# Decoder layer on one core: the order of SyncE's loads in three bodies, the first output chunks, and the last token block by halves

## What is computed

```python
h = rmsnorm(x, ln_gain[l])
z = jnp.einsum('bsd,de->bse', h, w_in[l])
q, k, v, g_attn, x_lru, g_lru = jnp.split(z, SPLITS, axis=-1)
q = partial_rope(q.reshape(b, s, N_Q_HEADS, HEAD_DIM), cos, sin)
k = partial_rope(k.reshape(b, s, N_KV_HEADS, HEAD_DIM), cos, sin)
...
y_attn = rmsnorm(y_attn * jax.nn.silu(g_attn), attn_out_gain[l])
u = causal_depthwise_conv(x_lru, conv_w[l], conv_b[l])
y_lru = rg_lru(u, w_rgate[l], b_rgate[l], w_igate[l], b_igate[l], lru_lambda[l])
y_lru = rmsnorm(y_lru * jax.nn.silu(g_lru), lru_out_gain[l])
y = jnp.einsum('bse,ed->bsd', jnp.concatenate([y_attn, y_lru], axis=-1), w_out[l])
x = x + y
...
return rmsnorm(x, final_gain)
```

## Time and profile before

| | |
|---|---|
| median of 3 runs | 1440.1 us (1439.48 to 1441.57) |
| profiled execution | 1439.82 us, span 1438.2 us |
| PE busy | 1380.8 us (96%), 6464 products |
| DVE / ACT / POOL busy | 1014.2 (71%) / 769.1 (53%) / 316.1 (22%) |
| clock granted to PE, mean | 0.993 |

### The profile page before, as it was taken

The page is one execution under the profiler, slowest core; times in us unless marked ns, Lnnn a source line. Parts: engine busy times, 40 slices in busy tenths (PEclk is TensorE's granted clock), DMA queues, the critical chain, the costliest instruction groups (busy, mean ns, idle before and its releaser), DMA issues.

```text
span 1438.2 us, 21776 instructions
## 1 busy us (share of the span) xinstructions
PE 1380.8 (96%) x6464; PEld 1136.5 (79%) x6464; DVE 1014.2 (71%) x1729; ACT 769.1 (53%) x1552; POOL 316.1 (22%) x317
## 2 busy tenths in 40 slices
PE   5999999799999999999999999999989999999997
PEld 4778777688888888888888878788868888888886
DVE  4798989687877778787787868777886644344443
ACT  5677685747475664747566564747575322222221
POOL 2131423042322314232231414232230000000000
PEclk9999999999999999999999999999999999999999
DMA  8767674755546454554636374544717323233220
GB/s 221 243 240 246 237 248 162 253 202 193 182 155 197 157 198 165 176 185 154 222 120 235 126 244 151 194 160 167 231 53 257 119 86 117 73 102 101 74 87 29
DMA packets 151726, 243.24 MB, mean 169 GB/s; under 512 B 35440, under 2 KB 101232, under 8 KB 151664
## 3 DMA queue, kind: packets, MB, share of 16 engines
q1 hardware_dynamic: 144496, 217.33, 45.4%
q0 software_dynamic: 7168, 25.17, 5.2%
HBM read 179.55 MB, written 62.91 MB: 169 GB/s over the span
## 4 chain that ended last, share of the span: by engine, by line
PE 43%; DVE 21%; issue 18%; ACT 8%; POOL 3%; DMA 2%; SPq 2%; DVEq 1%; ACTq 1%; POOLq 0%
PE ring L1408 18%; PE acc_b L201 12%; PE ring L201 11%; DVE hs L1283 5%; POOL ri L618 2%; DVE p_lo L1220 2%; ACT p_sb L834 2%; DVE s_sb L1194 2%; DVE smax L1207 1%; PE ps_v L1458 1%; DVE cu L1249 1%; DVE o_sb L1229 1%; ACT cu L858 1%; DVE w_lo L1002 1%; ACT kc_ol L847 1%
## 5 line engine op out<-in xcount | busy, mean ns | idle before, releaser
L1408 PE MATMUL ring<-split,w_hi 128*128 128x512 f32 x2304 | 720.3, 394 | 8.1 <-DVE split L1022 7.5
L1408 PEld LDWEIGHTS ring<-split,w_hi 128*128 128x128 f32 x2304 | 427.9, 189 | 95.6 <-DVE split L1022 8.4
L1408 PE MATMUL ring<-split,w_lo 128*128 128x512 f32 x1152 | 450.8, 391 | 0.0
L1408 PEld LDWEIGHTS ring<-split,w_lo 128*128 128x128 f32 x1152 | 217.2, 189 | 46.7
L834 ACT ACTIVATE p_sb<-s_sb,smax 128x129 f32<-128x129 f32 x256 | 99.9, 392 | 124.6 <-DVE smax L1207 124.4
L618 POOL TENSOR_TENSOR ri<-ri,hs 128x512 f32<-128x512 f32 x32 | 54.8, 1732 | 395.6 <-ACT hs L900 395.6
L774 ACT ACTIVATE q_st<-qrot 64x512 fp32r<-64x512 f32 x64 | 40.4, 631 | 114.9 <-DVE qrot L1085 114.1
L1249 DVE SCALAR_TENSOR_TENSOR cu<-xl,prm,cu 128x512 f32<-128x512 f32 x96 | 72.2, 752 | 39.6 <-ACT cu L858 30.6
L1669 ACT ACTIVATE w_hi<-res 128x1024 fp32r<-128x1024 f32 x16 | 17.0, 1061 | 144.5 <-DVE res L1728 144.5
L201 PE MATMUL ring<-split,y_own 128*128 128x512 f32 x384 | 91.3, 392 | 0.0
L201 PE MATMUL acc_b<-wo_rest,y_own 128*128 128x512 f32 x384 | 89.8, 390 | 0.5 <-DVE wo_rest L162 0.5
(11 more groups left out here) (195 smaller groups left out, 2486.0 us busy)
## 6 DMA issues: line engine op xcount, KB each, us to landing
w_hi<-w_split_scratch SPq DMA_DIRECT2D x108, 512.0 KB, 3.3
w_lo<-w_split_scratch SPq DMA_DIRECT2D x108, 512.0 KB, 4.3
w_split_scratch<-w_hi SPq DMA_DIRECT2D x36, 512.0 KB, 5.0
w_split_scratch<-w_lo SPq DMA_DIRECT2D x36, 512.0 KB, 5.7
w_raw<-w_in_d SPq DMA_DIRECT2D x32, 512.0 KB, 4.4
y_scratch<-hs POOLq DMA_DIRECT2D x32, 256.0 KB, 5.0
y_scratch<-ya POOLq DMA_DIRECT2D x16, 512.0 KB, 8.7
rows<-y_scratch SPq DMA_DIRECT2D x8, 1024.0 KB, 7.5
```

Source lines behind the costliest of these rows:

```text
L1408: last = mm(bank(r), w[:, i % WSLOTS, k, :], h[:, par, k, :], start=(k == 0 and j == 0), stop=(k == KC - 1 and j == 2))
```

## The change

Four things move. (1) In SP's list the four gate loads come directly behind XL1, ahead of `load_y(0, 0)` and the output weights; and the tables with their wait come behind GA0, GA1 and GL1. (2) In the four split bodies `norm_x` comes ahead of `softmax_a(1)` on DVE. (3) In the last body the gaps take three chunks of block 0, then the fourth and two of block 1, then two more of block 1: eight in place of six; phase B's beginning has two fewer. (4) The last step of phase B is taken out of the loops and its second block is worked by halves of 512 columns: the recurrence's product, the add, the square sum, the scaling and the store, which goes out from SP in two transfers and no longer from POOL. An unused split and square sum of a further y block, which the loop made in its last step, is gone with it.

```diff
@@ SP, phase A, body @@
                 load(XL1, COL_XL + P)
+                sp.wait_ge(*gw_low.at(n, 0))
+                for j, w in enumerate((w_rgate, w_igate)):
+                    for half in range(2):
...
+                                     ).then_inc(*gw_dma.one())
                 if q == NQUART - 1 and g == 0:
...
-                sp.wait_ge(*gw_low.at(n, 0))
-                for j, w in enumerate((w_rgate, w_igate)):
...
+                load(GA0, COL_GA)
+                load(GA1, COL_GA + P)
+                load(GL1, COL_GL + P)
                 if nxt_par != par and not last:
                     sp.wait_ge(*q_rot.at(n, 0))
                     load_tables((q + 1) * T)
-                load(GA0, COL_GA)
-                load(GA1, COL_GA + P)
-                load(GL1, COL_GL + P)
@@ DVE, phase A, body @@
                 if split:
                     split_w(n, GL1)
+                    norm_x(n, x_root.at(n, 1), x_rs, x_norm)
                 softmax_a(1)
                 if q < NQUART - 1:
-                    norm_x(n, x_root.at(n, 1), x_rs, x_norm)
+                    if not split:
+                        norm_x(n, x_root.at(n, 1), x_rs, x_norm)
@@ PE, phase A, last body @@
                     pe.wait_ge(*signals_b.y_low.at(0, 1))
-                    for e in range(2):
+                    for e in range(3):
                         pe.wait_ge(*signals_b.wo_low.at(e, 1))
                         proj.chunk(pe, ring, 0, e)
                 weigh_v(1)
...
-                    for e in range(2, 4):
-                        pe.wait_ge(*signals_b.wo_low.at(e, 1))
-                        proj.chunk(pe, ring, 0, e)
+                    pe.wait_ge(*signals_b.wo_low.at(3, 1))
+                    proj.chunk(pe, ring, 0, 3)
+
+                    pe.wait_ge(*ring_act.at(n, FREED_BY_ACT.index(R_I1) + 1))
+                    pe.wait_ge(*ring_dve.at(n, FREED_BY_DVE.index(R_GL1) + 1))
+                    pe.wait_ge(*signals_b.y_low.at(0, 2))
+                    for e in range(2):
+                        proj.chunk(pe, ring, 1, e)
                 weigh_v(2)
                 turn_p(3)
...
-                    for e in range(2):
+                    for e in range(2, 4):
                         proj.chunk(pe, ring, 1, e)
                 weigh_v(3)
@@ PE, phase B, beginning @@
             begin(4)
             begin(5)
-            for e in range(2, 4):
-                second(e)
-                begin(e + 4)
+            begin(6)
             second(4)
+            begin(7)
             second(5)
@@ phase B, last block: SP, ACT, DVE, PE @@
+            for h in range(2):
+                sp.wait_ge(b.half_normed, h + 1)
+                cols = slice(h * (D // 2), (h + 1) * (D // 2))
+                sp.dma_start(out[0, SEQ - P:, cols], res[:, 1, cols]).then_inc(b.half_out, 16)
+            sp.wait_ge(b.half_out, 32)
...
+            for h in range(2):
+                act.wait_ge(b.half_added, h + 1)
+                nc.scalar.activation(junk[:, h * (D // 2):(h + 1) * (D // 2)], res[:, 1, h * (D // 2):(h + 1) * (D // 2)],
+                                     ACT.Square, accum_out=stat[:, h, 0:1]).then_inc(b.half_sq, 1)
+            act.wait_ge(b.half_mean, 2)
...
+            for h, cols in enumerate(halves):
+                dve.wait_ge(b.half_product, h + 1)
+                stt(out=res[:, 1, cols], in0=acc_of(1, 1)[:, h, :], scalar=rms[:, 1, 2, 1:2], in1=res[:, 1, cols],
+                    op0=ALU.mult, op1=ALU.add).then_inc(b.half_added, 1)
...
+            step(STEPS - 1, 1, EC // 2)
+
+            pe.wait_ge(*b.y_mean.at(STEPS - 1, 4))
+            for h in range(2):
+                for e in range(EC // 2, EC):
+                    last = proj.multiply(pe, acc, 1, e, (h,))
+                last.then_inc(b.half_product, 1)
```

More of the change, by code:

```diff
@@ L195, in sum_y, with multiply @@
             ins.then_inc(*(self.b.y_part if half == 1 else self.b.y_tree).one())
-    def chunk(self, pe, banks, s, e):
+    def multiply(self, pe, banks, s, e, halves):
         g = e // (EC // 2)
         for j, (y, low) in enumerate(((self.y_hi, 0), (self.y_hi, 1), (self.y_lo, 0))):
-            for h in range(2):
+            for h in halves:
                 last = self.nc.tensor.matmul(banks[:, ACC[s, g][h], :], y[s][:, e, :],
@@ L204, in chunk @@
                                              stop=(e % (EC // 2) == EC // 2 - 1 and j == 2))
+        return last
+    def chunk(self, pe, banks, s, e):
+        last = self.multiply(pe, banks, s, e, range(2))
         if (e + 1) % (EC // 2) == 0:
@@ L1590, in signals_of_phase_b @@
     sem = lambda name: top.enter_context(nc.semaphore(name))
+    (b.half_product, b.half_added, b.half_sq, b.half_mean, b.half_root, b.half_normed, b.half_out) = (
+        sem("half_" + s) for s in ("product", "added", "sq", "mean", "root", "normed", "out"))
     b.over, b.fgain_in, b.settled = sem("phase_a_over"), sem("fgain_in"), sem("settled_b")
@@ L1767, in _, with step @@
             normalise(0, 1)
-            with dve.Fori(1, STEPS) as m:
-                for s in range(2):
-                    mean_y(m, s)
-                    proj.low_y(dve, m + s, 1 - s)
-                    rms_y(m, s)
-                    for g in range(2):
-                        proj.sum_y(dve, m + s, 1 - s, g)
-                    for g in range(2):
-                        add_group(m, s, g)
-                    normalise(m, s)
+            def step(m, s):
+                mean_y(m, s)
+                proj.low_y(dve, m + s, 1 - s)
+                rms_y(m, s)
+                for g in range(2):
+                    proj.sum_y(dve, m + s, 1 - s, g)
+                for g in range(2):
+                    add_group(m, s, g)
+                normalise(m, s)
+            with dve.Fori(1, STEPS - 1) as m:
+                for s in range(2):
+                    step(m, s)
+            m = STEPS - 1
+            step(m, 0)
+            mean_y(m, 1)
+            rms_y(m, 1)
+            add_group(m, 1, 0)
+            dve.wait_ge(*b.added.at(m, 3))
+            halves = [slice(h * (D // 2), (h + 1) * (D // 2)) for h in range(2)]
+            for h, cols in enumerate(halves):
+                dve.wait_ge(b.half_product, h + 1)
+                stt(out=res[:, 1, cols], in0=acc_of(1, 1)[:, h, :], scalar=rms[:, 1, 2, 1:2], in1=res[:, 1, cols],
+                    op0=ALU.mult, op1=ALU.add).then_inc(b.half_added, 1)
+                dve.wait_ge(b.half_sq, h + 1)
+                if h == 0:
+                    nc.vector.tensor_scalar(stat[:, 0, 1:2], stat[:, 0, 0:1], 1.0 / D, EPS, ALU.mult, ALU.add
+                                            ).then_inc(b.half_mean, 1)
+                else:
+                    dve.wait_ge(b.half_mean, 1)
+                    nc.vector.tensor_scalar(stat[:, 1, 1:2], stat[:, 1, 0:1], 1.0 / D, stat[:, 0, 1:2], ALU.mult, ALU.add
+                                            ).then_inc(b.half_mean, 1)
+            dve.wait_ge(b.half_root, 1)
+            nc.vector.reciprocal(stat[:, 1, 3:4], stat[:, 1, 2:3]).then_inc(b.half_root, 1)
+            dve.wait_ge(b.half_root, 2)
+            for cols in halves:
+                stt(out=res[:, 1, cols], in0=res[:, 1, cols], scalar=stat[:, 1, 3:4], in1=fgain[:, cols],
+                    op0=ALU.mult, op1=ALU.mult).then_inc(b.half_normed, 1)
         @block.tensor
```

69 lines of the change are left out of this document (36 added, 33 removed).

## The result

The changed kernel took 1425.04 us (median of four runs, 1424.16 to 1425.95) beside 1439.84 for the kernel before: ratio 0.990, 95% interval 0.9888 to 0.9912, or 14.8 us less. The forecast was 11.5 us less, 1428.6, with a range down to 1426.1. The kernel was measured again beside the last experiments: 1423.74 (1423.06 to 1426.38).

What follows compares the result with a forecast made beforehand. PE, busy 1380.8 of 1438.2 us, was taken as the bound, so its removed waits shorten the time. Terms -7.5 - 2.8 + 0.2 + 0.4 - 1.8 = -11.5 from 1440.1 gave 1428.6 us, range 1426.1 to 1432.8.

Steps and rivals of the forecast that it cites:

- part 5: Tail: last block by halves, stored from SP, shortens the end behind the last product; -1.8 us, bounds -1.0 and -2.3.
- part 2: Body 12: gate loads first remove PE's wait and slow clock, GA0's weights then slightly late; gain 2.8 us, bounds 1.2 and 4.1.
- part 1: Body 3: tables behind GA0, GA1 and GL1 remove two gate-product waits and the slow clock; -7.5 us, low end 5.9.
- Part 3: Split bodies: norm_x ahead of softmax_a(1) only moves PE's wait from turn_x to block 0's v product; +0.2 us.
- part 4: Last body: early chunks buy nothing and block 2's v product comes 0.4 later; +0.4 us, bounds -0.1 and +0.9.
- the 1.6 for the clock: Body 3: granted clock 0.73 over 6 us behind the long wait loses 1.6 us, which returns with the wait.
- (c): Bodies 3, 7 and 11: tables come too late, holding VectorE's first rotation and the key product; above 1443 us; 2%.
- (d): Body 3: GA0's load finds its slot still taken, ACT waits as before, gain 1 and not 7.5; 1435.1 us; 5%.
- small waits: Body 12: 0.5 us taken off the gain because bodies 13 to 15 show small waits at their v products.
- (b): Body 12: GA0's weights take the gate weights' place and eat the whole gain there; 1431.4 us; 15%.
- my own test: Split bodies: if block 0's v product does not wait longer (about 1.3 us), VectorE is not the bound there.
- (a): Last body: early chunks count if output weights come in time, giving -2.1 and not +0.4; 1426.1 us; 12%.

Runs made afterwards that it cites:

- alone: Kernel before with only one part of the change; parts 1 to 5 in order: 1431.5, 1436.79, 1439.7, 1441.04 and 1437.06 us.
- the kernel with the gate loads in the middle: Changed kernel, in body 12 the four gate loads behind load_y(0, 0) and ahead of the three output weights: 1424.98 us.

## Why the prediction was right or wrong

The time lies below the range because three terms of the sum were too small: part 5 by 1.5 us, part 2 by 1.4 and part 1 by 1.0. Part 3 had its sign wrong, and part 4 held.

**Part 1: right in cause and place, 1.0 too small.** Forecast -7.5, measured -8.45 alone. The waits to the first gate product gave 4.30 (forecast 4.14). Between the gate products went 3.63, where I had 1.95 - 0.21 + 1.6 = 3.34: I kept body 2's wait of 0.21 as a floor, and body 3 now has none (6.87 us between its gate products, 7.24 in body 2). And turn_x waits 0.70 and not 1.10, in a stretch that is 0.5 shorter, which I had not counted. One term was right by its sum and not by its reason: the 1.6 for the clock. In the seven profiles with the tables in their old place the stretch between the two gate products took 10.44 to 10.50 us, whether the clock in it was 0.71 or 0.85, with PE waiting 0.53 us or 1.95. DVE's u_lo sets this stretch, and a lower clock only fills the wait. Wait and lost clock together measure how late u_lo was, so the sum came out near; a "low end with no clock regained" had no ground. The kernel with the tail alone, with its wait of 0.53, to be laid beside the 10.50 us of the earlier trace rows:

```profile
264.94:275.38 10.44, 9.92 (x30) 7.59 (x30) 6.94 (x13) 8.47 (x14) 0.00 (x0) 0.71 0.74 277
```

The tables cost nothing, in bodies 7 and 11 either. Rivals (c) and (d) fall.

**Part 2: right in the wait, wrong in the step behind it.** Forecast -2.8, measured -4.16 alone and -4.26 in the whole: the full 2.42 + 1.7 that the earlier trace rows show. Here the clock's part was time: from the first gate product to the v product of block 3 body 12 took 45.44 before and 43.77 after. The step that failed is that the y load goes out about 2.5 us later, "so GA0 comes 0.1 to 2.2 us late; I take 0.8". GA0 came 1.2 us earlier against the work of PE (19.8 and not 21.0 behind the same v product). The y load did go out 2.6 us later, but I had carried its delay through to GA0: SP's issues behind it stood less (one took 3.81 us before, none over 1.3 after), so GA0 was issued 2.9 us earlier. Nor does an issue set the landing: in the kernel with the gate loads in the middle GA0 was issued 3.3 us later than in the changed kernel and landed 0.3 earlier. Nor did the 0.5 of "small waits" come off: bodies 13 to 15 have theirs as before, in either kernel, and body 12 none. Rival (b) has its mechanism, 0.41 us of wait in one profile of six, and not its price.

**Part 3: wrong in place and sign, small.** Forecast +0.2; measured -0.2 in each of bodies 1 to 3. The bounds were -0.2 and +0.9, and the three bodies gave -0.7. The wait did stay on the path, as I said, but at the score products and not at the v product: I had followed only what norm_x was moved past for PE's turn_x, and not that softmax_a(1)'s copy frees the bank of the next scores. The gain comes from a term that I didn't have, DVE's durations beside POOL. The v product did not wait longer, and by my own test that should have meant that DVE is not the bound; the test was wrong, since the same wait had been taken earlier.

**Part 4: right.** Forecast +0.4, measured +0.42 in the whole, +0.45 alone, -0.4 where it was undone. The v product of block 2 moved as forecast. The waits for output weights are 0.63 + 1.40 + 0.88 = 2.9, forecast 3.6. Rival (a) falls.

**Part 5: right in direction, sized at half.** Forecast -1.8, measured -3.3. The halves gave 0.85 (forecast 0.6 + 0.5 - 0.1 = 1.0). The issue gave 0.71 (forecast 0.55). The landing was forecast 2.7 and took 2.1: I had bounded SP by a load of 3.3 us taken in the loop, beside other transfers, and a lone store of the same size takes 2.6. And the largest miss is a term that stood in no line of the sum: the 1.3 us between the landing and the span's end, which I had in plain numbers (1433.97 + 2.9 = 1436.9, span 1438.2) and took as fixed. It went to 0.4 with SP's store.

**The sum.** -8.4 - 4.3 - 0.7 + 0.4 - 3.3 = -16.3 by the stretches, against -11.5. The profile of before had the shortest stretch of all from the last v product to the last product, 0.5 below that of after, and 0.1 less at the start, which leaves -15.6 of span and -14.8 of medians. Every term but part 4 was sized too cautiously, and its bounds on the fast side were too tight: all of them together reached 1425.9, and the range began at the price of rival (a), 1426.1.

## What to carry to other kernels

When a wait goes, read what is left between the two milestones around it and not only the bracket: the waits behind it shrink too, and an operation that is moved is also moved past the buffers that its new neighbours free. Small loads that an engine waits for belong ahead of the large ones: behind 2.5 MB ACT stood 8.06 us for them, behind 1 MB 0.78, and directly behind XL1 not at all; and look at the landing of what stands behind them, not at its issue. At the end of a program write out the whole sum from the last product to the span's end, the piece behind the last landing too, and ask of each piece which queue owns it.

## What the hardware showed that I had not expected

- The same waits are sometimes followed by a lower clock and sometimes not. Behind the 1.37 us in body 13 four of the fourteen profiles have a fall that costs 1.05 us, the others none. In the last body the stretch between two v products was 6.70 us with PE at a clock of 1.00 and a wait of 2.21, and 6.70 at 0.75 with a wait of 0.63: DVE sets it, and the lower clock only fills the wait. Windows of before and of the kernel with the tables moved alone:

```profile
1067.75:1074.45 6.70, 4.49 (x20) 3.29 (x21) 6.42 (x10) 3.66 (x11) 2.39 (x4) 1.00 0.00 0
```

```profile
1059.26:1065.96 6.70, 6.07 (x21) 4.53 (x21) 6.42 (x10) 3.65 (x11) 2.40 (x4) 0.75 0.01 2
```

- A scaling of 128x1024 on DVE took 1.29 us where it started 0.37 ahead of a product of POOL, and 2.37 where both started together; the product took 2.04 and 1.29. Between the two lies 1.50, started 0.87 behind a first product and 0.38 ahead of a second.
- SP's issue of a 32 KB load can stand for over 3 us behind a 1 MB load (two issues took 4.68 us, 1.25 elsewhere).
- A span ended 0.4 us behind the last landing where SP had stored last, and 0.9 to 1.3 behind it where POOL had.
